# Pool branch of a decoder layer: band matrices on TensorE against running sums on VectorE

## The chip, the cores and the metric

One core of a Trainium2 chip runs one launch of the kernel. The metric is device microseconds of one execution; the times given are medians of several.

## The reference

A trunk of two layers (DEPTH = 2) over 256 tokens and a width of 2048, all in float32. The part of a layer that matters here is the mixer: one input projection gives 1024 pool columns, 512 columns for q, 512 for kv and 64 for the key rope. The pool columns go through four causal means, one per group of 256 columns:

```
def multiscale_pool(u, pool_w, pool_scale):
    cs = jnp.cumsum(uf, axis=1)
    for g, w in enumerate((2, 4, 8, 16)):
        c = cs[..., g * POOL_C:(g + 1) * POOL_C]
        lag = jnp.pad(c, ((0, 0), (w, 0), (0, 0)))[:, :S]
        cnt = jnp.minimum(t + 1, w)
        outs.append((c - lag) / cnt)
    diff = pooled - u                      # per group
    y = einsum('bsgc,gcd->bsgd', diff, pool_w) * pool_scale

u = rms_norm(h, norm_mix_g[i]) @ w_in[i]
y_pool = multiscale_pool(u[..., :1024], ...)
y_att = latent_attention(u[..., 1024:1536], u[..., 1536:2048], u[..., 2048:], ...)
h = h + concat([y_pool, y_att]) @ w_out[i]
h = h + conv_gated_ffn(...);  h = h + (p[i] @ w_ple[i]) * sigmoid(...)
```

## The kernel before

Products are made in two parts: every weight and every activation is split into a rounded part (hi, fp32r) and the rest (lo), and three products hi x hi, lo x hi, hi x lo are summed in PSUM (`three`, lines 1607 to 1611).

**Weights.** SP loads chunks of 128x2048 into four slots. Each chunk is two halves of 128x1024. ScalarE rounds a half to `w_hi` (`split`, line 648, copy at L658), VectorE subtracts to `w_lo` (`split`, line 1075, L1085). `steps(l, a, b)` splits halves a + 4 to b + 3 of the layer; six halves are held, and a split waits until TensorE has used the half six before. `halves(l, m)` on TensorE waits for the low part of half m. The order of splits, evictions and everything else is written out by hand for each engine: what stands in between on VectorE or ScalarE delays the next split. Halves of a layer: 0 to 7 q latent, 8 to 19 kv latent and key rope, 20 to 27 and 28 to 35 pool, 36 and 37 q rope, 38 to 41 q, 42 to 45 k, 46 to 49 v, 50 and 51 pool_w, 52 to 83 w_out.

**PSUM.** `acc` is two tiles of two banks, taken in turn by blocks (`free_acc`, `block_split`); `tps` is four banks taken in turn by jobs (`new_job`, `jobs_split`).

**Two ways to run a projection.** By token (`square_half`, line 1627): activations 128x128 are stationary, weights of 512 columns move, 96 products of 512 columns in a block of 512 outputs. By row of weights (`by_rows`, line 1963, the gate and up blocks of the FFN): weights 128x128 are stationary, and both parts of the activations of 256 tokens move in one product of 512 columns (`wide`, L1971), the low weights in one of 256 (`half`, L1981); 64 of each in a block. There the normed scale of a token is a row, made by transposing (`rows_spread`).

**The pool branch.** Both pool blocks run by token. `pooled(i)` evicts a block: ScalarE scales by the token's norm factor and rounds (L800), VectorE subtracts (L1097). `diffs(i)` on TensorE (line 1753) multiplies the block by band matrices, which hold mean minus identity for each window: five products for each of four feature tiles (L1766 to L1770). ScalarE rounds the result (L808) and VectorE subtracts (L1096). The first `diffs` stands after two halves of the second pool block, the second after the q projection. GpSimd builds the bands at the start (lines 522 to 537) and finishes them in `band_parts` (line 550).

**Order on TensorE around it:** key rope block, five halves of pool block 0, transposes of the key rope and of the kv latent (10), three halves, two halves of pool block 1, `diffs(0)`, six halves, q rope (`qrope`), q (`qnope`), `diffs(1)`, k (`knope`), transposes of q rope, v, then scores of head 0, `pool_out`, and the heads. Before the scores TensorE waits for the eviction of the first v block (`block_split(l, BL["v"])`, line 1895).

**Order on VectorE from the q block on:** eviction of q (two blocks, `qk`), splits 44 and 45, `diffs(1)`, splits 46 and 47, eviction of k (two blocks), splits 48 and 49, four subtractions of the q rope, splits 50 and 51, eviction of v (two blocks, two subtractions each), splits 52 and 53, softmax of head 0.

Of the kernel before, what the change touches and what calls it, by code (L numbers as in the profile page):

```python
# [27 lines left out]
P = 128  # L28
F32 = mybir.dt.float32
# [3 lines left out]
ALU = mybir.AluOpType  # L33
# [12 lines left out]
POOL_SETUP = 44 + 4 * len(POOL_WINDOWS) + 4 * len(POOL_WINDOWS)  # L46
# [11 lines left out]
def layer_plan(d_model, d_ff):  # L58
# [26 lines left out]
    for name, n in (("cq", 1), ("pool", 2)):  # L85
        for i in range(n):
            last[block[name] + i] = 2 * (chunk[name] + (i + 1) * per_block) - 1
    last[block["ckv"]] = 2 * chunk["ckr"] + 5
# [33 lines left out]
def build(nc, x, p, positions, norm_mix_g, w_in, pool_w, pool_scale, q_norm_g, w_uq, kv_norm_g, w_ukv,  # L122
# [26 lines left out]
    TURNS = JOBS - (ROWS_JOBS - 1) - FFN_JOBS - (P_JOBS - 1)  # L149

    def turned(l, job):

        n = job
        for name, skipped in (("rows", ROWS_JOBS - 1), ("ffn", FFN_JOBS), ("p", P_JOBS - 1)):
            if job > JB[name]:
                n -= skipped
        return TURNS * l + (n + 1)
# [12 lines left out]
    with ExitStack() as ctx:  # L170
# [11 lines left out]
        band_lo = sb("band_lo", [P, len(POOL_WINDOWS), 16], F32R)  # L182
# [16 lines left out]
        band_hi = sb("band_hi", [P, len(POOL_WINDOWS), 3 * P], F32R)  # L199
# [15 lines left out]
        with ExitStack() as scope:  # L215
# [3 lines left out]
            band = sb("band", [P, len(POOL_WINDOWS), 3 * P], scope=scope)  # L219
            inv_cnt = sb("inv_cnt", [P, 16], scope=scope)  # L220
# [7 lines left out]
        with ExitStack() as scope:  # L228
# [12 lines left out]
            with ExitStack() as early:  # L241
                up_ = (sb("upool_hi", [P, TT, BLK], F32R, scope=early),
                       sb("upool_lo", [P, TT, BLK], F32R, scope=early))
# [56 lines left out]
        upool_hi = sem("upool_hi")  # L300
        diff_hi = sem("diff_hi")
        qr_step = sem("qr_step")
# [38 lines left out]
        STEPS = 4 + 2 + 2 + 4 + 5  # L341

# [155 lines left out]
        def _(pool):  # L498
# [26 lines left out]
            pool.wait_ge(dve_setup, 1)  # L525
            for g, w in enumerate(POOL_WINDOWS):
                step(pool.tensor_copy(band[:, g, 0:w], inv_cnt[:, 0:w]))
            after()
            for g, w in enumerate(POOL_WINDOWS):
                for c0, cn in ((0, 2 * P), (2 * P, P)):  # L530
                    b = band[:, g, c0:c0 + cn]
                    step(pool.affine_select(out=b, in_=b, compare_op=ALU.is_ge, fill=0.0, base=0,
                                            pattern=[[1, cn]], channel_multiplier=-1))
                    after()
                    step(pool.affine_select(out=b, in_=b, compare_op=ALU.is_ge, fill=0.0, base=w - 1,
                                            pattern=[[-1, cn]], channel_multiplier=1))
            after()
# [11 lines left out]

            def band_parts():  # L550
                for g in range(len(POOL_WINDOWS)):
                    for c0 in (0, 2 * P):
                        step(pool.tensor_tensor(band[:, g, c0:c0 + P], band[:, g, c0:c0 + P], ident[:, :],
                                                ALU.subtract))
                after()

                step(pool.tensor_copy(band_hi[:, :, :], band[:, :, :]))
                after()
                step(pool.tensor_tensor(band_lo[:, :, :], band[:, :, 0:16], band_hi[:, :, 0:16].bitcast(F32),
                                        ALU.subtract))  # L560
                assert n[0] == POOL_SETUP
# [24 lines left out]
            for l in range(L):  # L586
# [4 lines left out]
                if l == 0:  # L591
                    band_parts()
# [43 lines left out]
        def _(act):  # L636
# [84 lines left out]
            for l in range(L):  # L721
# [74 lines left out]
                def pooled(i):  # L796
                    b = BL["pool"] + i
                    block_ready(act, l, b)
                    for t in range(TT):
                        copy(up_[0][:, t, :], acc[b % 2][:, t, :], ACT.Copy,  # L800
                             scale=rstd["mix"][:, t:t + 1]).then_inc(upool_hi, 1)

                def diffs(i):
                    for k in range(2):
                        job = JB["diff"] + 2 * i + k
                        act.wait_ge(t_ready, turned(l, job))
                        kt = DIFF + 4 * i + 2 * k
                        copy(xb[0][:, kt:kt + 2, :].rearrange("p a b -> p (a b)"), tps[:, job % T_BANKS, :],  # L808
                             ACT.Copy).then_inc(diff_hi, 1)

                pooled(0)
                steps(l, 28, 30)
                diffs(0)
                steps(l, 30, 36)
# [14 lines left out]
                steps(l, 40, 42)  # L829
                diffs(1)  # L830
                steps(l, 42, 44)
# [3 lines left out]
                for i in range(2):  # L835
# [4 lines left out]
                    copy(q_both[ROPE:P, 2 * i:2 * i + 2, 1, :], pair[ROPE:P], ACT.Copy).then_inc(qr_hi, 1)  # L840
                steps(l, 46, 48)
# [206 lines left out]
        def _(dve):  # L1048
# [17 lines left out]

            step(dve.memset(k_lo[ROPE:P, 0, :].bitcast(F32), 0.0))
# [87 lines left out]
            for l in range(L):  # L1155
# [48 lines left out]
                dve.wait_ge(kr_step, 3 * l + 2)  # L1204
                dve.tensor_copy(kr_tok[:, :, ROPE:P], kr_tok[:, :, 0:ROPE]).then_inc(kr_step, 1)
# [4 lines left out]
                bank = tps[:, JB["kr"] % T_BANKS, 0:S]  # L1210
                lo(k_lo[0:ROPE, 0, :], bank[0:ROPE], k_hi[0:ROPE, :])
# [4 lines left out]

                def pooled(i):
                    b = BL["pool"] + i
                    for t in range(TT):
                        dve.wait_ge(upool_hi, 2 * TT * l + TT * i + t + 1)  # L1220
                        lo(up_[1][:, t, :], acc[b % 2][:, t, :], up_[0][:, t, :],
                           rstd["mix"][:, t:t + 1]).then_inc(acc_free[b % 2], 1)

                def diffs(i):
                    for k in range(2):
                        job = JB["diff"] + 2 * i + k
                        dve.wait_ge(diff_hi, 4 * l + 2 * i + k + 1)
                        kt = DIFF + 4 * i + 2 * k
                        two = lambda x: x[:, kt:kt + 2, :].rearrange("p a b -> p (a b)")
                        lo(two(xb[1]), tps[:, job % T_BANKS, :], two(xb[0])).then_inc(t_done, 1)  # L1230
# [3 lines left out]
                diffs(0)  # L1234
                steps(l, 30, 36)
# [36 lines left out]
                diffs(1)  # L1272
# [3 lines left out]
                steps(l, 44, 46)  # L1276
# [8 lines left out]
                steps(l, 46, 48)  # L1285
# [311 lines left out]
        def _(pe):  # L1597
# [91 lines left out]
            for l in range(L):  # L1689
# [54 lines left out]
                square_halves(l, m, b, xa, 0, 5)  # L1744
                pe.wait_ge(kr_step, 3 * l + 3)
                bank = new_job(l, JB["kr"])
                for t in range(TT):
                    ins = pe.transpose(bank[:, t * P:(t + 1) * P], kr_tok[:, t, :], ident[:, :])
# [4 lines left out]
                def diffs(i):  # L1753

                    if i == 0:
                        pe.wait_ge(pool_setup, POOL_SETUP)
# [393 lines left out]
```

## Time and profile before

| what | value |
|---|---|
| median of 3 runs | 2195.02 us (2194.47 to 2195.32) |
| the profiled execution's own time | 2194.54 us |
| its span, first to last instruction | 2192.8 us |
| TensorE busy | 2180.4 us, 11639 products |
| VectorE busy | 1475.3 us |
| ScalarE busy | 1045.6 us |
| GpSimd busy | 61.7 us |
| granted TensorE clock, mean | 0.999 |

The times in the rows count from the start of the span. In a timeline a row is a run of like instructions: start, length, engine, line, operation, tiles, shape, count, and in brackets the idle time before it with what ended it. Products overlap: one of 512 columns is shown with 0.39 us, but the next starts about 0.227 us after it, so the cost of a run is read from the starts.

### The profile page before, as it was taken

How to read it: one execution, taken by the hardware profiler on the slowest of the kernel's cores; microseconds unless marked ns; L12 is line 12 of the kernel's file. 1: busy time of each engine (PE TensorE's matmuls, PEld its weight loads, DVE VectorE, ACT ScalarE, POOL GpSimd, SP SyncE). 2: the span in 40 equal slices, each digit the busy share in tenths (PEclk: the TensorE clock that was granted, in tenths of full speed). 3: DMA queues.
4: the chain of work that ended last, by engine and by line, in shares of the span. 5: the costliest groups of instructions: out<-in, count | busy, mean ns of one | idle time of the engine just before them, and what ended most of it. 6: DMA issues, size and time to landing. Idle time of an engine off the chain costs nothing.

```text
span 2192.8 us, 32099 instructions
## 1 busy us (share of the span) xinstructions
PE 2180.4 (99%) x11639; PEld 1888.9 (86%) x11639; DVE 1475.3 (67%) x1852; ACT 1045.6 (48%) x1338; POOL 61.7 (3%) x144
## 2 busy tenths in 40 slices
PE   9999999999999999999999999999999999999998
PEld 8898888888888888888898988888888888888886
DVE  6577567766677766676556765677666677766764
ACT  6555444444444443445554554444443444444554
POOL 5000000000000000000000000000000000000011
PEclk9999999999999999999999999999999999999999
DMA  7644555555555555555556355555555555555562
GB/s 258 204 148 154 192 191 182 195 185 191 191 192 191 191 191 188 195 172 193 189 171 187 131 177 184 186 194 189 191 191 191 191 191 191 188 183 189 181 217 96
DMA packets 232987, 406.44 MB, mean 185 GB/s; under 512 B 14780, under 2 KB 49708, under 8 KB 232792
## 3 DMA queue, kind: packets, MB, share of 16 engines
q1 hardware_dynamic: 231824, 402.68, 55.4%
q0 software_dynamic: 512, 1.76, 0.3%
q10 hardware_dynamic: 584, 1.11, 0.1%
q8 instruction: 42, 0.69, 0.1%
q14 instruction: 25, 0.20, 0.0%
HBM read 403.42 MB, written 2.10 MB: 185 GB/s over the span
## 4 chain that ended last, share of the span: by engine, by line
PE 99%; issue 0%; DVE 0%; ACT 0%; POOL 0%; POOLq 0%; ACTq 0%
PE acc L1971 15%; PE tps L1971 15%; PE acc L1609 14%; PE acc L1611 14%; PE acc L1610 14%; PE tps L1981 8%; PE acc L1981 8%; PE tps L1610 4%; PE tps L1611 4%; PE tps L1609 4%; PE tps L1666 1%; PE tps L1602 0%; PE tps L1875 0%; DVE w_lo L1085 0%; PE tps L1855 0%
## 5 line engine op out<-in xcount | busy, mean ns | idle before, releaser
L1085 DVE TENSOR_TENSOR w_lo<-raw,w_hi 128x1024 fp32r<-128x1024 f32 (+1 forms) x768 | 920.3, 1218 | 450.9 <-ACT w_hi L913 309.2
L913 ACT ACTIVATE w_hi<-raw 128x1024 fp32r<-128x1024 f32 x508 | 529.4, 1059 | 664.4 <-PE acc L1971 129.7
L1971 PE MATMUL acc<-xa,w_hi 128*128 128x512 f32 x1408 | 333.5, 390 | 0.0
L658 ACT ACTIVATE w_hi<-raw 128x1024 fp32r<-128x1024 f32 (+1 forms) x260 | 262.1, 1042 | 147.9 <-PE acc L1611 143.0
L1971 PE MATMUL tps<-xa,w_hi 128*128 128x512 f32 x1408 | 331.1, 390 | 0.0
L1971 PEld LDWEIGHTS tps<-xa,w_hi 128*128 128x128 f32 x1408 | 261.5, 188 | 52.4
L1971 PEld LDWEIGHTS acc<-xa,w_hi 128*128 128x128 f32 x1408 | 260.8, 188 | 52.3 <-DVE h L1350 0.4
L1609 PE MATMUL acc<-w_hi,xb_hi 128*128 128x512 f32 x560 | 220.7, 394 | 0.0
L1611 PE MATMUL acc<-w_lo,xb_hi 128*128 128x512 f32 x560 | 218.2, 390 | 0.0
L1610 PE MATMUL acc<-w_hi,xb_lo 128*128 128x512 f32 x560 | 217.8, 389 | 0.0
L1981 PEld LDWEIGHTS acc<-xa,w_lo 128*128 128x128 f32 x1408 | 175.5, 191 | 3.9
L1981 PEld LDWEIGHTS tps<-xa,w_lo 128*128 128x128 f32 x1408 | 174.7, 192 | 3.4
L1981 PE MATMUL acc<-xa,w_lo 128*128 128x256 f32 x1408 | 176.7, 283 | 0.0
L1981 PE MATMUL tps<-xa,w_lo 128*128 128x256 f32 x1408 | 175.8, 283 | 0.0
L1609 PE MATMUL acc<-w_hi,xa 128*128 128x512 f32 (+1 forms) x384 | 139.5, 363 | 1.5 <-DVE xa L1097 1.5
L1611 PE MATMUL acc<-w_lo,xa 128*128 128x512 f32 (+1 forms) x384 | 137.7, 359 | 0.0
L1610 PE MATMUL acc<-w_hi,xa 128*128 128x512 f32 (+1 forms) x384 | 137.4, 358 | 0.0
L1609 PE MATMUL acc<-w_hi,gt_hi 128*128 128x512 f32 x320 | 124.5, 389 | 0.0
L1610 PE MATMUL acc<-w_hi,gt_lo 128*128 128x512 f32 x320 | 124.5, 389 | 0.0
L1611 PE MATMUL acc<-w_lo,gt_hi 128*128 128x512 f32 x320 | 124.5, 389 | 0.0
L1609 PE MATMUL tps<-w_hi,gt_hi 128*128 128x512 f32 x320 | 124.5, 389 | 0.0
L1610 PE MATMUL tps<-w_hi,gt_lo 128*128 128x512 f32 x320 | 124.5, 389 | 0.0
(224 smaller groups left out, 2499.9 us busy)
## 6 DMA issues: line engine op xcount, KB each, us to landing
raw<-in_w_up SPq DMA_DIRECT2D x176, 1024.0 KB, 4.9
raw<-in_w_down SPq DMA_DIRECT2D x88, 1024.0 KB, 4.9
raw<-in_w_out SPq DMA_DIRECT2D x32, 1024.0 KB, 5.0
raw<-in_w_ple_gate SPq DMA_DIRECT2D x32, 1024.0 KB, 4.9
raw<-in_w_in SPq DMA_DIRECT2D x22, 1024.0 KB, 5.3
raw<-in_w_ukv SPq DMA_DIRECT2D x8, 1024.0 KB, 5.4
raw<-in_w_in SPq DMA_DIRECT2D x8, 864.0 KB, 4.8
raw<-in_w_uq SPq DMA_DIRECT2D x6, 1024.0 KB, 5.6
```

What stands on the lines that cost most here:

```text
L658: copy(w_hi[:, half_of(m), 0:n], raw[:, c % RAW_SLOTS, at:at + n], ACT.Copy).then_inc(hi_done, 1)
L913: copy(w_hi[:, half_of(m), :], raw[:, c % RAW_SLOTS, (m % 2) * HALF:(m % 2 + 1) * HALF], ACT.Copy).then_inc(hi_done, 1)
L1085: dve.tensor_tensor(w_lo[:, half_of(m), 0:n], raw[:, c % RAW_SLOTS, at:at + n], w_hi[:, half_of(m), 0:n].bitcast(F32), ALU.subtract).then_ ...
L1609: pe.matmul(dst, a_hi, b_hi, start=first, stop=False)
L1610: pe.matmul(dst, a_lo, b_hi, start=False, stop=False)
L1611: return pe.matmul(dst, a_hi, b_lo, start=False, stop=last)
L1666: ins = pe.transpose(bank[:, i * S + t * P:i * S + (t + 1) * P], tiles(t, i), ident[:, :])
L1971: ins = pe.matmul(dst, hi[:, k * BLK + n * P:k * BLK + (n + 1) * P], x_both[:, kt, :, :].rearrange("p a s -> p (a s)"), start=kt == 0, sto ...
L1981: ins = pe.matmul(bank(n, False)[:, S:2 * S], lo[:, k * BLK + n * P:k * BLK + (n + 1) * P], xa[0][:, kt, :], start=False, stop=False)
```

## The change

TensorE now runs both pool blocks by row of weights: the left one (halves 20 to 27) in the four banks of `acc`, the right one (28 to 35) in the four banks of `tps`. The result has features on partitions and tokens along the row. The norm factors come as a row: VectorE spreads the factor of each token over a 128x128 tile, two more transposes turn them, and `mix_row` keeps them. `pooled(i)` copies the low sums on ScalarE and adds the high sums on VectorE into `u_pool[i]`, with 16 zeroed columns ahead of the tokens. `by_mix_row(i)` multiplies by the factors. `windows(i, k)` doubles a running sum by additions of a shifted copy (one addition for window 2, two for 4, three for 8, four for 16), corrects the first tokens, and takes u from the scaled sum. `diffs(i, k)` rounds on ScalarE and subtracts on VectorE as before, from SBUF. Band matrices, band products and `band_parts` go. Before `pool_out` TensorE waits for all four differences. On VectorE, `windows(1, 1)` stands between the splits of halves 48 and 49, and the subtractions of the right half's differences between 50 and 51.

```
TensorE
-                square_halves(l, m, b, xa, 0, 5)
+                by_rows(m, left_bank, 0, 6, None, 2)
                 pe.wait_ge(kr_step, 3 * l + 3)
...
+                for t in range(TT):
+                    ins = pe.transpose(bank[:, S + t * P:S + (t + 1) * P], u_pool[1][:, t, PAD:PAD + P], ident[:, :])
                 turn_lat(1, JB["ckv"])
-                square_halves(l, m, b, xa, 5, 8)
-                square_halves(l, m, b, xa, 0, 2)
-                diffs(0)
-                square_halves(l, m, b, xa, 2, 8)
+                by_rows(m, left_bank, 6, 8)
+                by_rows(m + 8, right_bank, 0, 8)
...
                 by_feature(m, BL["qnope"], LAT_Q)
-                diffs(1)
                 jobs_split(l, JB["ckv"] + 1)
...
                     if i == 0:
+                        pe.wait_ge(diff_lo, 4 * l + 4)
                         pool_out(0)

by_rows, first two halves of the left block
+                        if cautious == 2 and i == 0:
+                            for j in range(2):
+                                halves(l, m + j, v)
+                            for ns in ((0, 1), (2, 3)):
+                                for j in range(2):
+                                    wide(j, ns)
+                                    ins = half(j, ns)

ScalarE
+                        for k in range(2):
+                            block_ready(act, l, b)
+                            copy(u[:, 2 * k:2 * k + 2, :], acc[b % 2][:, :, S:2 * S], ACT.Copy).then_inc(u_lo, 1)
+                    else:
+                        halves_used(act, l, 2 * CH["pool"] + 15)
+                        copy(u[:, 0:3, :], tps[:, 1:4, S:2 * S], ACT.Copy).then_inc(u_lo, 1)
+                        copy(u[:, 3, :], tps[:, 0, S:2 * S], ACT.Copy).then_inc(u_lo, 1)
...
                 pooled(0)
-                steps(l, 28, 30)
-                diffs(0)
-                steps(l, 30, 36)
+                steps(l, 28, 33)
+                diffs(0, 0)
+                diffs(0, 1)
+                steps(l, 33, 36)
...
-                steps(l, 40, 42)
-                diffs(1)
-                steps(l, 42, 44)
+                steps(l, 40, 44)
...
+                diffs(1, 0)
+                diffs(1, 1)
                 steps(l, 46, 48)

VectorE
+                for t in range(TT):
+                    dve.tensor_scalar(u_pool[1][:, t, PAD:PAD + P], ident[:, :], 0.0, rstd["mix"][:, t:t + 1], ...)
+                dve.tensor_copy(mix_row[:, :], tps[:, JB["kr"] % T_BANKS, S:2 * S]).then_inc(win_step, 1)
...
+                def windows(i, k):
+                    w = POOL_WINDOWS[2 * i + k]
+                    src, shift, flip = u, 1, 0
+                    while shift < w:
+                        win_ready()
+                        win_next(dve.tensor_tensor(to[:, :, PAD:PAD + S], src[:, :, PAD:PAD + S],
+                                                   src[:, :, PAD - shift:PAD + S - shift], ALU.add))
+                        src, shift, flip = to, 2 * shift, 1 - flip
+                    win_ready()
+                    win_next(dve.scalar_tensor_tensor(first, first, float(w), inv_cnt[:, 0:w]..., ALU.mult, ALU.mult))
+                    win_ready()
+                    dve.scalar_tensor_tensor(u[:, :, PAD:PAD + S], src[:, :, PAD:PAD + S], 1.0 / w,
+                                             u[:, :, PAD:PAD + S], ALU.mult, ALU.subtract).then_inc(diff_done, 1)
...
                 pooled(0)
                 steps(l, 28, 30)
-                diffs(0)
-                steps(l, 30, 36)
+                by_mix_row(0)
+                windows(0, 0)
+                steps(l, 30, 31)
+                windows(0, 1)
+                steps(l, 31, 33)
+                diffs(0, 0)
+                diffs(0, 1)
+                steps(l, 33, 36)
                 pooled(1)
                 steps(l, 36, 38)
...
                 steps(l, 40, 42)
-                diffs(1)
+                by_mix_row(1)
+                windows(1, 0)
                 steps(l, 42, 44)
                 qk(BL["knope"], K_T, 4)
                 qk(BL["knope"] + 1, K_T + 4, 6)
-                steps(l, 44, 46)
+                steps(l, 44, 45)
+                windows(1, 1)
+                steps(l, 45, 46)
...
-                steps(l, 46, 48)
+                steps(l, 46, 47)
+                diffs(1, 0)
+                diffs(1, 1)
+                steps(l, 47, 48)

GpSimd
-            for g, w in enumerate(POOL_WINDOWS):
-                step(pool.memset(band[:, g, :], 1.0 / w))
...
+            pool.wait_ge(x_landed[1], 16)
             with nc.allow_non_contiguous_dma(reason="256 positions, once"):
                 pool.dma_start(pos_i[:, :], ...)
...
-                if l == 0:
-                    band_parts()
```

## Rows read from the trace of the kernel before

**Rows 1.** The page: busy time by engine, and the chain that ended last by engine

```profile
PE 2180.4 (99%) x11639; PEld 1888.9 (86%) x11639; DVE 1475.3 (67%) x1852; ACT 1045.6 (48%) x1338; POOL 61.7 (3%) x144
...
PE 99%; issue 0%; DVE 0%; ACT 0%; POOL 0%; POOLq 0%; ACTq 0%
```

**Rows 2.** Stretches: length, busy time of PE, PEld, DVE, ACT, POOL, clock, DMA share, GB/s

```profile
62.68:109.75 47.07, 47.07 (x224) 39.46 (x223) 26.45 (x35) 22.89 (x33) 1.08 (x3) 1.00 0.69 208
...
76.31:77.40 1.09, 1.09 (x11) 1.09 (x10) 0.26 (x1) 0.58 (x2) 0.00 (x0) 1.00 0.05 17
...
91.11:93.34 2.23, 2.23 (x22) 2.22 (x20) 0.31 (x1) 0.60 (x1) 0.00 (x0) 1.00 0.53 143
...
126.71:128.94 2.23, 2.23 (x23) 2.23 (x21) 1.29 (x2) 2.03 (x4) 0.00 (x0) 1.00 0.03 10
...
1149.18:1196.25 47.07, 47.07 (x224) 39.47 (x223) 26.46 (x35) 22.89 (x33) 1.08 (x3) 1.00 0.66 188
```

**Rows 3.** Timeline of TensorE: k products, fourth half of v, first scores

```profile
130.90 0.28 PE L1610 MATMUL acc<-xb_hi,w_lo 128*128 128x256 f32 x1
131.02 0.28 PE L1611 MATMUL acc<-xb_lo,w_hi 128*128 128x256 f32 x1
131.39 0.38 PE L1609 MATMUL acc<-xb_hi,w_hi 128*128 128x256 f32 x1
...
145.87 0.40 PE L1609 MATMUL acc<-w_hi,xb_hi 128*128 128x512 f32 x1
...
152.69 0.22 PE L1609 MATMUL tps<-xa 128*128 128x128 f32 x1
```

**Rows 4.** Timeline of ScalarE after the q products

```profile
126.91 1.09 ACT L824 ACTIVATE xa<-acc 128x512 fp32r<-128x512 f32 x2 [4.67 <-PE acc L1611]
127.88 2.01 ACT L658 ACTIVATE w_hi<-raw 128x1024 fp32r<-128x1024 f32 x2
```

**Rows 5.** Timeline of VectorE from the q products to the eviction of v

```profile
128.97 2.36 DVE L1085 TENSOR_TENSOR w_lo<-raw,w_hi 128x1024 fp32r<-128x1024 f32 x2
...
143.10 2.36 DVE L1085 TENSOR_TENSOR w_lo<-raw,w_hi 128x1024 fp32r<-128x1024 f32 x2
...
150.73 1.29 DVE L1096 TENSOR_TENSOR v_lo<-acc,v_hi 128x512 fp32r<-128x512 f32 x2
```

**Rows 6.** Timeline of TensorE: gate and up blocks of the FFN's first unit

```profile
265.61 1.07 PE L1971 MATMUL acc<-xa,w_hi 128*128 128x512 f32 x4
...
271.46 1.03 PE L1666 MATMUL tps<-ident,h 128*128 128x128 f32 x8
272.25 2.07 PE L1971 MATMUL acc<-xa,w_hi 128*128 128x512 f32 x8
...
289.31 3.79 PE L1971 MATMUL tps<-xa,w_hi 128*128 128x512 f32 x16
...
311.53 0.84 PE L1971 MATMUL acc<-xa,w_hi 128*128 128x512 f32 x3
```

**Rows 7.** VectorE by line and shape, 62 to 153 us: busy us, mean ns

```profile
L1085 DVE TENSOR_TENSOR w_lo<-raw,w_hi 128x1024 fp32r<-128x1024 f32 x29 | 34.6, 1222 | 9.5 <-ACT w_hi L658 8.9
...
L1097 DVE SCALAR_TENSOR_TENSOR upool_lo<-acc,rstds,upool_hi 128x512 fp32r<-128x512 f32 x4 | 2.8, 747 | 7.6 <-ACT upool_hi L800 7.6
...
L1096 DVE TENSOR_TENSOR xb_lo<-tps,xb_hi 128x512 fp32r<-128x512 f32 x4 | 2.7, 686 | 3.0 <-ACT xb_hi L808 3.0
```

**Rows 8.** Timeline of VectorE: key rope, the third row waits for the second

```profile
63.78 0.22 DVE L1199 TENSOR_TENSOR kr_tok<-kr_in,cos 128x64 f32<-128x64 f32 x1
63.91 0.22 DVE L1200 TENSOR_TENSOR kr_tmp<-kr_in,sin 128x64 f32<-128x64 f32 x1
64.16 0.22 DVE L1202 TENSOR_TENSOR kr_tok<-kr_tok,kr_tmp 128x64 f32<-128x64 f32 x1
```

**Rows 9.** Timeline of TensorE: warm-up and first product

```profile
2.12 5.68 PE L1602 MATMUL tps<-ident 128*128 128x128 f32 x32 [2.12 <-POOL ident L514]
...
10.45 0.50 PE L1609 MATMUL acc<-w_hi,xa 128*128 128x512 f32 x1 [1.47 <-DVE xa L1097]
```

More of the change, by code:

```diff
@@ L87, in layer_plan @@
             last[block[name] + i] = 2 * (chunk[name] + (i + 1) * per_block) - 1
+    for i in range(2):
+        last[block["pool"] + i] = 2 * chunk["pool"] + 7
     last[block["ckv"]] = 2 * chunk["ckr"] + 5
@@ L148, in build @@
     FFN_JOBS = JB["p"] - JB["ffn"]
-    TURNS = JOBS - (ROWS_JOBS - 1) - FFN_JOBS - (P_JOBS - 1)
+    POOL_JOBS = 4
+    TURNS = JOBS - POOL_JOBS - (ROWS_JOBS - 1) - FFN_JOBS - (P_JOBS - 1)
     def turned(l, job):
         n = job
-        for name, skipped in (("rows", ROWS_JOBS - 1), ("ffn", FFN_JOBS), ("p", P_JOBS - 1)):
+        for name, skipped in (("diff", POOL_JOBS), ("rows", ROWS_JOBS - 1), ("ffn", FFN_JOBS), ("p", P_JOBS - 1)):
             if job > JB[name]:
@@ L241, in build @@
             with ExitStack() as early:
-                up_ = (sb("upool_hi", [P, TT, BLK], F32R, scope=early),
-                       sb("upool_lo", [P, TT, BLK], F32R, scope=early))
+                u_pool = [sb(f"u_pool{i}", [P, 4, PAD + S], scope=early) for i in range(2)]
             prob = sb("prob", [P, 2, 3 * P], scope=scope)
@@ L341, in build @@
         STEPS = 4 + 2 + 2 + 4 + 5
+        WIN_STEPS = 1 + 2 * (2 + 1) + sum(w.bit_length() for w in POOL_WINDOWS)
         def half_of(m):
@@ L548, in _ @@
                     lat_landed, 16)
[L550 to L561, printed above, removed]
             def factor(done, src, dst, n_terms, step0, halved=False):
@@ L796, in pooled, with diffs @@
                 def pooled(i):
[L797 to L809, printed above, removed]
+                    u = u_pool[i][:, :, PAD:PAD + S]
+                    if i == 0:
+                        for k in range(2):
+                            b = BL["pool"] + k
+                            block_ready(act, l, b)
[4 more added lines that the diff above has]
+                        copy(u[:, 3, :], tps[:, 0, S:2 * S], ACT.Copy).then_inc(u_lo, 1)
+                def diffs(i, k):
+                    act.wait_ge(diff_done, 4 * l + 2 * i + k + 1)
+                    kt = DIFF + 4 * i + 2 * k
+                    copy(xb[0][:, kt:kt + 2, :], u_pool[i][:, 2 * k:2 * k + 2, PAD:PAD + S], ACT.Copy).then_inc(
+                        diff_hi, 1)
                 pooled(0)
-                steps(l, 28, 30)
-                diffs(0)
-                steps(l, 30, 36)
+                steps(l, 28, 33)
+                diffs(0, 0)
+                diffs(0, 1)
+                steps(l, 33, 36)
                 pooled(1)
@@ L1215, in _ @@
                 steps(l, 26, 28)
-                def pooled(i):
[L1218 to L1224, printed above, removed]
-                    for k in range(2):
[L1226 to L1230, printed above, removed]
+                n_win = [WIN_STEPS * l + 1]
@@ L1745, in _, with left_bank, right_bank @@
+                def left_bank(n, first):
+                    if first and n % 2 == 0:
+                        free_acc(l, BL["pool"] + n // 2)
+                    return acc[(BL["pool"] + n // 2) % 2][:, n % 2, :]
+                def right_bank(n, first):
+                    assert JB["diff"] % T_BANKS == 1
+                    return new_job(l, JB["diff"] + n) if first else tps[:, (JB["diff"] + n) % T_BANKS]
+                by_rows(m, left_bank, 0, 6, None, 2)
                 pe.wait_ge(kr_step, 3 * l + 3)
```

196 lines of the change are left out of this document (107 added, 89 removed).

## The prediction

> **What bounds the kernel now.** I read the busy shares first: TensorE is busy 99% of the span, and the chain of waits lies on it for 99% too [rows 1]. So only two things change the time: what TensorE issues, and when it must wait. Every other engine counts only where TensorE waits for it. Next I read the stretches around the change. The pool columns, from the first of their weight halves to the first product with w_uq, take 47.07 us in either layer [rows 2], with TensorE busy throughout, so what holds for one layer is counted twice. In it lie the ten transposes of the key rope and the latent rows (1.09) and the first pair of band products (2.23); the second pair, 2.23 again, stands between the q and k projections [rows 2]. Last I read one engine at a time where TensorE reaches weights that VectorE has barely finished [rows 3 to 5]: there a moved instruction can cost.
>
> A measurement of this kernel can tell some 0.2%, or 4.4 us, from no change.
>
> **Step 1: columns by feature instead of by token.** Each block of 512 pool columns now runs as the gate and up blocks do: 64 products of 512 columns and 64 of 256, in place of 96 of 512. The columns streamed are equal. Before, the 16 halves cost 47.07 - 1.09 - 2.23 = 43.75 us. The up block of the first unit takes 311.53 - 289.31 = 22.22 [rows 6]; that is the right block. The left one has the order of the first gate block, which changes often between the two widths; that took 289.31 - 265.61 = 23.70, of which the eight transposes are 272.25 - 271.46 = 0.79, so 22.9 at most. As that still holds two more transposes and a wait for VectorE, I take 22.4. Sum 44.6, which is 0.87 more per layer (bounds 0.7 to 1.4). Two more transposes for the row of norm factors: 0.1 each, 0.2 in all.
>
> **Step 2: no band products before w_uq.** 2.23 us less per layer [rows 2]. Steps 1 and 2 give -2.23 + 0.87 + 0.2 = -1.15 per layer, -2.3 in all.
>
> **Step 3: no band products between q and k.** Here I take nothing, though 2.23 us of products go. The k projection uses halves 42 to 45 of its weights in its first 2.9 us. Halves 44 and 45 are split late: ScalarE first evicts the last q block (from 126.91), which waits for the end of the q products, and only then rounds 44 and 45 (127.88 to 129.89) [rows 4]; VectorE subtracts them from 128.97 to 131.33 [rows 5]. TensorE reaches half 45 at 131.39, after a gap of 0.37 between starts where 0.12 is usual [rows 3]: it waits for that half already. Without the band products it starts the k projection at 126.71, does halves 42 and 43, and waits for 44 and 45, which hang on the end of q by the same chain. The fourth half starts 4.68 us after the end of q either way. Bounds: 0 to -2.5 per layer (the 2.23 and the wait); I take 0, since both ends of this chain are in the rows.
>
> **Step 4: the window sums on VectorE.** Those of the left half (windows 2 and 4) run beside the right block. VectorE is busy 26.45 of the 47.07 us [rows 2]; the change adds some 6.5 us net, by the durations of [rows 7], and follows each piece by splits that TensorE uses at least 5 us later (half 34, the nearest, is ready about 9 us into the right block and used after 16). I cost this at nothing; if that cover failed, each late us would be a us of TensorE. The evictions of the right block hold up halves 40 and 41, ready about 5 us after the right block and used after 7. Window 8 stands before the eviction of the first k block, which then ends some 2 us later than now, still 2 us before v takes its bank.
>
> Window 16 does not fit. It stands on VectorE between the splits of halves 48 and 49, the last two of the v weights. Now 48 and 49 end at 143.10 + 2.36 = 145.46 [rows 5], and TensorE starts half 49's products at 145.87 [rows 3]: 0.4 us to spare. Inserted are four additions of 128x512, one small product for the first 16 tokens and one scaled subtraction of 128x512. A 128x512 subtraction takes 0.686, a scaled one 0.747 [rows 7]. Each addition waits for the one before. The price of such a wait is in [rows 8]: two independent steps start 0.13 apart (63.78, 63.91), a dependent one 0.25 after the step before it, its 0.22 and 0.03 more. So 4 x (0.69 + 0.03) + 0.25 + 0.67 = 3.80 us; the last is not waited for by split 49. Half 49 is then ready at 149.26, TensorE starts at 149.32 (0.06 after, as it did at 131.39) and waits **3.45 us**. The bounds: steps that overlap as independent ones, 0.6 apart, give 3.15; steps slower by a fifth give 4.5. I take 3.80, since the rows are of the same operation and size.
>
> The Trainium skill ("VectorE: DVE Perf Modes", section "The DRAIN you can't avoid") says that a semaphore after each of a chain of Vector operations costs nothing extra; by it the insertion would be about 3.2 us and the whole change +5.1 us in place of +6.4. The 0.25 against 0.13 of [rows 8] speaks against it here.
>
> What is late next: the v products end at 152.69 + 3.45 = 156.14, and TensorE then waits for the eviction of the first v block before the scores. VectorE ended that at 150.73 + 1.29 = 152.02, which is 6.56 us after split 49, with four subtractions and splits 50 and 51 between. The two subtractions of the right half's differences come in among these, 0.6 us each: 149.26 + 6.56 + 1.2 + 0.06 = 157.08, so TensorE waits **0.9 us** more (bounds 0 to 1.3). Queued behind is softmax of the first head; VectorE comes to it 3.8 + 1.2 later at most and TensorE 4.35 later, with pool products of 5.8 us between, so I count nothing.
>
> Per layer 3.45 + 0.9 = 4.35, twice 8.7.
>
> **Step 5: costed at nothing.** GpSimd builds no bands. Its set-up lay beside TensorE's warm-up, and the first product waited for VectorE's part of xa, not for bands [rows 9]; the cleared pads on VectorE fall into its wait for the first gains. GpSimd's six small transfers now wait for the second piece of x instead of for the bands, the piece that TensorE itself needs for its next transposes, and are used only after the first block. No weight transfer is moved on SP's queue; those behind half 49 start 3.8 us later, with chunks two ahead in hand.
>
> **Sum.** -2.3 + 0 + 8.7 = **+6.4 us**. The profiled execution took 2194.54 (span 2192.8), 0.48 under the median of 2195.02; its sum is 2200.9, and on the median's scale **2201.4**.
>
> **Rivals.**
> *The wait at half 49 costs little (not slower).* Its place is the gap between split 48 and TensorE's start on 49; it decides at an insertion of some 2.8 us: below that the two waits of a layer stay under 3.35 us and the time under +4.4. For it: in every other stretch VectorE stands idle and could absorb this. Against: six operations at [rows 7]'s prices do not fit under 3.1. Fully hidden it gives 2195.0 - 2.3 = 2192.7. Chance 0.18, for an order I misjudged.
> *All band products pay (faster).* If ScalarE rounds 44 and 45 before q ends and window 16 hides, 2 x 2.5 more goes: 2187.7. Against it is the chain of [rows 4, 5]. Chance 0.07.
> *TensorE slows after its waits.* After 1.47 us of idling it ran its next products at their usual pace [rows 9]; a wait of 3.45 us stands nowhere in the trace. The 32 transposes of the warm-up took 5.68 us, where 32 at the 0.1 of [rows 6] take 3.2: 2.5 lost at the lower pace. Twice that on top gives 2206.4. Chance 0.08. The Trainium skill ("TensorE: Matmul & The Clock Gate", section "Why this matters for your kernels") warns that idle gaps between bursts bring the clock back to half rate.
> *The windows 2, 4 or 8 hold up a split as well.* One late half of 1 to 3 us a layer: 2203 to 2207. Chance 0.05.
>
> **Numbers.** The forecast has 0.62. Its own range: low with an insertion of 3.15 or no second wait (+4.6 to +5.1), high with 4.5 (+8): 2199.4 to 2203.5. To leave out no more than 2 in 10 the range must take in the hidden case, 2192.0, and reach some way into the last two, 2205.0. Faster by over 0.2%: the second rival and a little, 0.08. Within 0.2%: the first rival, and the forecast's lowest corner, 0.24. Slower: 0.68.
>
> **What would show it.** Right: pool blocks of 22.2 to 22.5 us with no gap between; TensorE idle some 2 us and again 0.4 inside the first k products; idle of about 3.4 us at the fourth half of v, released by VectorE's split; about 0.9 us before the first scores. Wrong: half 49 split before TensorE gets to it, or k products that start their fourth half less than 4.5 us after q; or idle in the right pool block.

## The result and the profile after

The changed kernel takes **2205.11 us** (median of 5 runs, 2203.89 to 2206.00) against 2194.47 us of the kernel before (5 runs beside them): ratio 1.0048, 95% interval 1.0037 to 1.0058. The forecast was 2201.4 us; the direction was right, the time came out 3.7 us longer, just above the range's upper end. The kernel before ran at 2194.47 this time and not at 2195.02, so the change cost 10.6 us where 6.4 were forecast.

The page of the profiled execution (span 2204.1 us) first: busy time by engine, and the chain that ended last. Against [rows 1] VectorE has 24 us more, and 1% of the chain each now lies on VectorE and on issue.

```profile
PE 2181.5 (99%) x11691; PEld 1892.6 (86%) x11691; DVE 1499.3 (68%) x1903; ACT 1044.7 (47%) x1338; POOL 45.2 (2%) x110
...
PE 98%; issue 1%; DVE 1%; ACT 0%; POOL 0%; POOLq 0%; ACTq 0%; DVEq 0%
```

TensorE's waits of the whole span. The first row is new; the other two stand in the kernel before too.

```profile
PE acc L1655 <- DVE w_lo L1069: 10.4, 5, 3.2
PE tps L1648 <- POOL ident L522: 2.1, 1, 2.1
PE acc L1655 <- DVE xa L1081: 1.5, 1, 1.5
```

Stretches of the changed kernel, columns as in [rows 2]; the column to read is the one behind POOL, the granted clock, where 1.00 is the upper of the two levels (2.4 GHz) and 0.50 the lower (1.2 GHz).

```profile
63.20:109.20 46.00, 46.00 (x271) 40.70 (x269) 31.41 (x48) 22.54 (x33) 1.08 (x3) 1.00 0.70 211
...
127.47:129.69 2.22, 0.28 (x3) 0.08 (x1) 2.08 (x4) 2.22 (x3) 0.00 (x0) 1.00 0.01 4
129.69:133.60 3.91, 3.91 (x19) 3.73 (x20) 3.74 (x5) 1.53 (x2) 0.00 (x0) 0.57 0.38 98
...
146.33:149.93 3.60, 0.40 (x3) 0.01 (x1) 3.43 (x7) 2.44 (x5) 0.00 (x0) 1.00 0.00 0
149.93:154.20 4.27, 4.27 (x12) 3.37 (x13) 4.18 (x6) 2.45 (x4) 0.00 (x0) 0.60 0.69 238
154.20:158.49 4.29, 4.29 (x21) 3.51 (x20) 3.40 (x5) 0.00 (x0) 0.00 (x0) 1.00 0.21 47
1221.00:1223.80 2.80, 2.16 (x11) 1.96 (x12) 2.70 (x4) 2.00 (x3) 0.00 (x0) 0.76 0.03 5
1223.80:1226.50 2.70, 2.70 (x17) 2.70 (x16) 2.56 (x5) 0.00 (x0) 0.00 (x0) 0.61 0.92 309
...
1238.30:1241.90 3.60, 0.40 (x2) 0.00 (x0) 3.43 (x7) 2.44 (x5) 0.00 (x0) 1.00 0.01 2
1241.90:1246.40 4.50, 4.49 (x13) 3.57 (x14) 4.41 (x6) 2.47 (x4) 0.00 (x0) 0.62 0.70 233
```

The pool stage is 1.07 us shorter. Then come, in each layer, two stretches with TensorE nearly idle (2.22 and 3.60 us), and behind each of the four a stretch in which it is busy at a clock of 0.57 to 0.76 (the row at 1221.00 still holds the last 0.48 us of its wait). What a fall costs TensorE is its length times the missing share: 3.91 x 0.43 = 1.68, 4.27 x 0.40 = 1.71, 2.80 x 0.24 + 2.70 x 0.39 = 1.72, 4.50 x 0.38 = 1.71. It is 1.7 us each time.

Both places on TensorE's timeline: the end of q and half 45 in k, then half 49 in v and the first scores. The bracket gives the idle time; behind it the starts, 0.23 apart at 146, lie 0.43 apart from 150.74 on.

```profile
126.15 0.28 PE L1655 MATMUL acc<-xb_hi,w_hi 128*128 128x256 f32 x1
...
130.83 0.58 PE L1655 MATMUL acc<-xb_hi,w_hi 128*128 128x256 f32 x1
...
146.10 0.39 PE L1656 MATMUL acc<-w_hi,xb_lo 128*128 128x512 f32 x1
146.33 0.40 PE L1657 MATMUL acc<-w_lo,xb_hi 128*128 128x512 f32 x1
149.93 0.50 PE L1655 MATMUL acc<-w_hi,xb_hi 128*128 128x512 f32 x1 [3.20 <-DVE w_lo L1069]
...
150.74 0.63 PE L1655 MATMUL acc<-w_hi,xb_hi 128*128 128x512 f32 x1
151.17 0.63 PE L1656 MATMUL acc<-w_hi,xb_lo 128*128 128x512 f32 x1
151.59 0.63 PE L1657 MATMUL acc<-w_lo,xb_hi 128*128 128x512 f32 x1
...
158.49 0.22 PE L1655 MATMUL tps<-xa 128*128 128x128 f32 x1
```

VectorE at that time, answering to the row at 143.10 of [rows 5]: the split of half 48, the window of 16, the split of half 49, and further down the eviction of v's first block.

```profile
143.78 1.23 DVE L1069 TENSOR_TENSOR w_lo<-raw,w_hi 128x1024 fp32r<-128x1024 f32 x1
144.93 0.69 DVE L1247 TENSOR_TENSOR win<-u_pool 128x512 f32<-128x512 f32 x1
145.65 2.14 DVE L1247 TENSOR_TENSOR win<-win 128x512 f32<-128x512 f32 x3
147.82 0.19 DVE L1252 SCALAR_TENSOR_TENSOR win<-win,inv_cnt 128x32 f32<-128x32 f32 x1
148.05 0.69 DVE L1256 SCALAR_TENSOR_TENSOR u_pool<-win,u_pool 128x512 f32<-128x512 f32 x1
148.66 1.22 DVE L1069 TENSOR_TENSOR w_lo<-raw,w_hi 128x1024 fp32r<-128x1024 f32 x1
...
156.34 1.29 DVE L1080 TENSOR_TENSOR v_lo<-acc,v_hi 128x512 fp32r<-128x512 f32 x2
```

The insertion lasts from 144.93 to 148.66, 3.73 us, and the split of half 49 ends at 149.88, 0.05 before TensorE goes on.

To compare executions I counted from each one's first product of 512 columns, because that moves from run to run (last experiment). Each entry is a start on TensorE's timeline less that of this product: the first transpose of q's rope part (the end of the k products), the first v product and the first scores. The kernels' names are those of the experiments below.

| us from the first product to | before | changed | window_early | splits_early | filled | before_splits_early | v_first |
|---|---|---|---|---|---|---|---|
| end of k, layer 0 | 130.38 | 130.55 | 130.42 | 126.72 | 129.39 | 130.06 | 126.73 |
| first v product, layer 0 | 131.17 | 131.34 | 131.21 | 127.51 | 130.18 | 130.85 | 127.52 |
| scores, layer 0 | 142.24 | 147.52 | 143.09 | 140.86 | 145.66 | 141.84 | 138.99 |
| scores, layer 1 | 1228.76 | 1239.53 | 1230.89 | 1227.57 | 1235.61 | 1227.93 | 1222.29 |
| (first product at) | 10.45 | 10.97 | 10.73 | 9.99 | 11.13 | 10.18 | 11.08 |

Both layers lose about the same: 5.28 us up to the first scores of layer 0, 10.77 up to those of layer 1, so 5.49 in layer 1. With the later start (0.52) that is the 11.3 us between the spans.

### The profile page after: what moved, and what is told of

It is laid out like the page before. It is cut to its first block, busy times and chain, and to the rows that moved or that the text cites. A ratio compares the mean times of both kernels' runs of the same rounds, so it can differ in the third digit from the quotient of the medians.

```text
span 2204.1 us, 32232 instructions
## 1 busy us (share of the span) xinstructions
PE 2181.5 (99%) x11691; PEld 1892.6 (86%) x11691; DVE 1499.3 (68%) x1903; ACT 1044.7 (47%) x1338; POOL 45.2 (2%) x110
## 4 chain that ended last, share of the span: by engine, by line
PE 98%; issue 1%; DVE 1%; ACT 0%; POOL 0%; POOLq 0%; ACTq 0%; DVEq 0%
PE acc L1799 16%; PE tps L1799 16%; PE acc L1655 12%; PE acc L1657 12%; PE acc L1656 12%; PE tps L1809 8%; PE acc L1809 8%; PE tps L1657 4%; PE tps L1656 4%; PE tps L1655 4%; PE tps L1712 1%; PE tps L1648 0%; DVE win L1247 0%; PE tps L1971 0%; DVE w_lo L1069 0%
## 5 line engine op out<-in xcount | busy, mean ns | idle before, releaser
L1799 PE MATMUL acc<-xa,w_hi 128*128 128x512 f32 x1536 | 366.0, 391 | 0.0
L1799 PE MATMUL tps<-xa,w_hi 128*128 128x512 f32 x1536 | 361.2, 390 | 0.0
L1799 PEld LDWEIGHTS tps<-xa,w_hi 128*128 128x128 f32 x1536 | 285.3, 188 | 57.2
L1799 PEld LDWEIGHTS acc<-xa,w_hi 128*128 128x128 f32 x1536 | 283.7, 188 | 56.2 <-DVE h L1396 0.4
L1809 PEld LDWEIGHTS acc<-xa,w_lo 128*128 128x128 f32 x1536 | 192.7, 191 | 5.1
L1809 PE MATMUL acc<-xa,w_lo 128*128 128x256 f32 x1536 | 194.2, 283 | 0.0
L1809 PE MATMUL tps<-xa,w_lo 128*128 128x256 f32 x1536 | 191.8, 283 | 0.0
L1655 PEld LDWEIGHTS acc<-w_hi,xb_hi 128*128 128x128 f32 x560 | 105.9, 189 | 28.6 <-DVE w_lo L1069 7.6
L1657 PEld LDWEIGHTS acc<-w_lo,xb_hi 128*128 128x128 f32 x560 | 106.0, 189 | 22.6
L1657 PE MATMUL tps<-w_lo,gt_hi 128*128 128x512 f32 x320 | 124.5, 389 | 0.0
```

Source lines behind the costliest of these rows:

```text
L1655: pe.matmul(dst, a_hi, b_hi, start=first, stop=False)
L1657: return pe.matmul(dst, a_hi, b_lo, start=False, stop=last)
L1799: ins = pe.matmul(dst, hi[:, k * BLK + n * P:k * BLK + (n + 1) * P], x_both[:, kt, :, :].rearrange("p a s -> p (a s)"), start=kt == 0, sto ...
L1809: ins = pe.matmul(bank(n, False)[:, S:2 * S], lo[:, k * BLK + n * P:k * BLK + (n + 1) * P], xa[0][:, kt, :], start=False, stop=False)
```

## Experiments

Theory A: the loss is TensorE's two waits in each layer **and** the fall of the granted clock behind each. Rivals: VectorE bounds the stage, so a wait only changes place (B); the products are slow for another reason than the idling, the new VectorE work or the layout (C).

**Window 16 out of the gap (window_early).** VectorE does it where it stood idle:

```
                 qk(BL["knope"], K_T, 4)
-                qk(BL["knope"] + 1, K_T + 4, 6)
-                steps(l, 44, 45)
                 windows(1, 1)
...
-                steps(l, 45, 46)
+                qk(BL["knope"] + 1, K_T + 4, 6)
+                steps(l, 44, 46)
```

> The changed kernel with one move: VectorE does the window of 16 between the evictions of the two blocks of k, where it stood idle for 3.79 us, and no longer between the splits of halves 48 and 49. Theory A (TensorE's idle stretches and the low granted clock behind each make the loss): the wait at half 49 (3.4 us a layer) and the 1.7 us at a granted clock of 0.60 behind it go, twice; VectorE still has the copies of the pool differences ahead of v's first block, so some 0.6 us a layer of waiting come up before the scores: 2205.1 - 2 x (3.4 + 1.7 - 0.6) = 2196, and the granted clock around v is 1.00; around k it still falls to about 0.57. Rival B (VectorE is the bound of the stage, and the 3.7 us are only pushed to another wait): a wait of 2 us or more turns up at k's second block or before the scores, and the time stays above 2202.

Measured: 2197.43 us, ratio to before 1.0012 (1.0003 to 1.0021). The wait at half 49 and the fall behind it are gone in both layers, and the first scores of layer 0 come 4.43 us sooner than in the changed kernel. Of the loss 7.7 us come back, not 9: the wait before the scores took 1.04 between starts, 0.8 more than usual, where 0.6 was expected. Around k the clock still falls in both layers. B is out for this wait. The stretch around v and the wait before the scores, layer 0:

```profile
142.00:153.00 11.00, 11.00 (x50) 8.77 (x48) 10.56 (x15) 8.72 (x13) 0.00 (x0) 1.00 0.28 95
```

```profile
153.82 0.30 PE L1654 MATMUL tps<-xa 128*128 128x128 f32 x1 [0.66 <-DVE v_lo L1080]
```

**The splits too (splits_early).** As above, and on both engines halves 44 and 45 ahead of q's second block, 48 and 49 ahead of k's second (VectorE shown, ScalarE alike):

```
                 qk(BL["qnope"], Q_T, 0)
+                steps(l, 40, 42)
                 qk(BL["qnope"] + 1, Q_T + 4, 2)
-                steps(l, 40, 42)
...
                 windows(1, 1)
...
+                steps(l, 44, 46)
                 qk(BL["knope"] + 1, K_T + 4, 6)
-                steps(l, 44, 46)
```

> As window_early, and ScalarE and VectorE split halves 44 and 45 ahead of the eviction of q's second block, and 48 and 49 ahead of that of k's second block. Theory A: the waits at halves 44 and 45 (together 2.3 us a layer) and the 1.7 us at the low clock behind them go too, and the 0.6 us before the scores: 2196 - 2 x (2.3 + 1.7 + 0.6) = 2187, no granted clock under 0.95 between 109 and 160 us, below both kernels. Rival B: the splits can't start earlier, since they need halves 38 and 39 (42 and 43) used, which comes only at the end of the group before; then the later evictions cost as much as the earlier splits give, and the time is that of window_early, 2196.

Measured: 2193.03 us, ratio 0.9993 (0.9984 to 1.0002), a miss of 6 us. The k stage did what A said (end of k 3.83 us earlier than in the changed kernel, clock 1.00). The scores then met part of what B names, a late eviction: VectorE's of v's first block, still behind splits and differences. TensorE's timeline, and the stretches behind that wait, layer 0 and layer 1:

```profile
148.73 0.39 PE L1657 MATMUL acc<-w_lo,xb_hi 128*128 128x512 f32 x1
150.85 0.30 PE L1655 MATMUL tps<-xa 128*128 128x128 f32 x1 [1.73 <-DVE v_lo L1081]
```

```profile
150.85:155.00 4.15, 4.15 (x24) 4.15 (x25) 4.04 (x9) 1.28 (x2) 0.00 (x0) 0.65 0.69 246
...
1238.00:1243.00 5.00, 5.00 (x44) 5.00 (x44) 3.87 (x10) 1.98 (x5) 0.00 (x0) 1.00 0.65 222
```

The wait is the same in both layers, the fall comes in one only.

**TensorE kept at work while it waits (filled).** The waits stay; transposes that nobody reads fill them:

```
+                def fill(job, count):
+                    for _ in range(count):
+                        pe.transpose(tps[:, job % T_BANKS, 0:P], ident[:, :], ident[:, :])
...
+                                    if k in fills:
+                                        new_job(l, JB["qrope"])
+                                        fill(JB["qrope"], fills[k])
                                     parts.append(halves(l, m + k))
...
-                by_feature(m, BL["knope"], LAT_KV)
+                by_feature(m, BL["knope"], LAT_KV, {2: 16, 3: 3})
...
+                            if k == 3:
+                                new_job(l, JS[0])
+                                fill(JS[0], 28)
                             parts.append(halves(l, m + k))
```

> The changed kernel with the waits left where they are, and TensorE given transposes of the identity that nobody reads while it waits: 16 ahead of half 44 and 3 ahead of half 45 in k, 28 ahead of half 49 in v. Nothing of the chains of ScalarE and VectorE changes. Theory A (the clock falls because TensorE stood idle): the groups of halves 44, 45 and 49 begin when they did, but the granted clock behind them stays at 1.00: 4 x 1.7 us come back, and of them 2 x 0.9 go into the wait before the scores that was forecast: 2205.1 - 6.8 + 1.8 = 2200. Rival C (the products are slow for another reason, such as VectorE and ScalarE working on the same memory, or operands that came late): the products behind the waits stay at 0.213 and 0.427 us, and the time at 2205.

Measured: 2201.9 us, ratio 1.0032 (1.0020 to 1.0044). The v place again:

```profile
145.32 0.39 PE L1657 MATMUL acc<-w_lo,xb_hi 128*128 128x512 f32 x1
145.55 3.22 PE L1892 MATMUL tps<-ident 128*128 128x128 f32 x28
148.94 0.50 PE L1655 MATMUL acc<-w_hi,xb_hi 128*128 128x512 f32 x1 [0.16 <-DVE w_lo L1069]
149.28 0.39 PE L1656 MATMUL acc<-w_hi,xb_lo 128*128 128x512 f32 x1
149.50 0.40 PE L1657 MATMUL acc<-w_lo,xb_hi 128*128 128x512 f32 x1
149.74 0.39 PE L1655 MATMUL acc<-w_hi,xb_hi 128*128 128x512 f32 x1
...
156.79 0.30 PE L1655 MATMUL tps<-xa 128*128 128x128 f32 x1 [0.76 <-DVE v_lo L1080]
```

```profile
129.46:134.00 4.54, 4.34 (x36) 4.03 (x35) 4.37 (x6) 1.99 (x3) 0.00 (x0) 1.00 0.37 97
...
149.00:153.00 4.00, 4.00 (x18) 3.31 (x19) 3.91 (x6) 2.40 (x4) 0.00 (x0) 1.00 0.68 232
```

Half 49's products still begin 3.62 us after the product before the fill, VectorE and ScalarE have the same work, and the products behind run 0.23 apart at a clock of 1.00. So the idling brings the fall; C is out. The gain, 3.2 us, is less than the 6.8 that four falls cost, and less than the 5 expected, for two reasons that the rows show: part of the fall in k lies ahead of half 45, for which TensorE waits anyhow (end of k 1.16 us earlier, not 1.7), and the wait before the scores, foretold at 0.9, appears (1.14 between starts), because the products no longer run late.

**The kernel before without its second band products (before_no_cover, no_cover_again).**

```
+                            if i == 1:
+                                ins = pe.matmul(d[:, 0:16], up_[0][:, 0, f], band_lo[:, g, :], start=True, stop=True)
+                                continue
```

> The kernel before, with the second set of band products (between q and k) cut to one product of 16 columns for each bank: the differences of the last two windows are not computed. Less work for TensorE by 2.2 us a layer, and nothing else changed. Theory A: halves 44 and 45 arrive when they did, so the group of half 45 still begins 4.68 us after the end of q; TensorE stands idle for some 2 us in between, and the granted clock falls behind that: 1.7 us a layer slower with less work, 2194.5 + 3.4 = 2198. Rival C (the fall has to do with the new VectorE work or the by-feature layout): no fall, 2194.5. Rival D (the products did hold up the path after all): 2194.5 - 4.4 = 2190.

> The kernel of before_no_cover once more, unedited: its only trace had idle stretches of 1.78 us and no fall, at 2194.5, while its ten other runs took 2195.4 to 2196.8. Theory A: those are runs with a fall in one layer (1.2 us behind half 45); a second trace with a time near 2196 shows one granted clock near 0.6 behind half 44 or 45, one near 2194.5 shows none. Rival F (they are slower for another reason): a time near 2196 and a granted clock of 1.00 throughout.

Measured: 2196.24 us (11 runs, 2194.51 to 2196.76), ratio 1.0007 (0.9998 to 1.0016); the second traced execution took 2195.69. In the first trace (2194.51 us) both layers wait 1.78 us between starts without a fall, and the end of k, 130.47 us after the first product, is within 0.1 us that of the kernel before. In the second the wait is the same, and in layer 0, not in layer 1, the clock falls; k ends there at 131.91, 1.44 later:

```profile
129.93 0.39 PE L1609 MATMUL acc<-xb_hi,w_hi 128*128 128x256 f32 x1 [1.50 <-DVE w_lo L1085]
131.07 0.39 PE L1609 MATMUL acc<-xb_hi,w_hi 128*128 128x256 f32 x1 [0.16 <-DVE w_lo L1085]
```

```profile
132.00:134.00 2.00, 2.00 (x12) 2.00 (x11) 2.00 (x3) 0.43 (x1) 0.00 (x0) 0.50 0.79 256
...
1219.00:1221.00 2.00, 1.93 (x16) 1.93 (x17) 2.00 (x4) 1.44 (x2) 0.00 (x0) 1.00 0.37 67
```

Two things follow. Taking 2.2 us of products a layer off TensorE there gains nothing, as the forecast's third step said (D is out). And the fall comes without any of the change's VectorE work. It did not come every time, so A's 2198 was too high.

**The same with a longer wait (before_longer_wait).** On ScalarE, in the kernel without those products:

```
-                steps(l, 40, 42)
                 diffs(1)
-                steps(l, 42, 44)
+                steps(l, 40, 44)
```

> The kernel before with the second set of band products cut as in before_no_cover, and ScalarE's two copies of the last two differences moved ahead of its copies for halves 44 and 45, so that these come 0.95 us later: TensorE's idle stretch ahead of half 44 grows from 1.7 to about 2.6 us. In before_no_cover the profiled execution showed no fall of the granted clock behind 1.78 us and took just the time of the kernel before, while the timed ones lay up to 2.3 us higher. Theory A (the fall comes from the idle stretch, and a longer one makes it likelier): a granted clock near 0.6 behind the wait in both layers, and 2194.6 + 2 x (0.95 + 1.2) = 2199. Rival C (only the by-feature kernel has it): granted clock 1.00, and 2194.6 + 2 x 0.95 = 2196.5.

Measured: 2198.58 us, ratio 1.0020 (1.0011 to 1.0029): near A's 2199, and 2.1 above C's. In the trace the fall is again in one layer, not in both, behind equal waits:

```profile
132.05 0.38 PE L1608 MATMUL acc<-xb_hi,w_hi 128*128 128x256 f32 x1 [2.47 <-DVE w_lo L1084]
...
1219.51 0.49 PE L1608 MATMUL acc<-xb_hi,w_hi 128*128 128x256 f32 x1 [2.48 <-DVE w_lo L1084]
```

```profile
133.00:135.00 2.00, 1.83 (x16) 1.81 (x16) 2.00 (x4) 0.58 (x1) 0.00 (x0) 1.00 0.34 39
...
1221.00:1223.00 2.00, 2.00 (x12) 2.00 (x11) 2.00 (x4) 0.03 (x1) 0.00 (x0) 0.50 0.49 120
```

Counted from the first product, k ends 0.98 us later than in the kernel before in the layer without the fall, which is the longer wait, and another 2.02 later in the layer with it. So the fall itself brought 1.04 here, and A's number was met in part by luck: another 0.8 of the traced execution is its late start (first product at 11.28).

**A version without the waits (v_first).** As splits_early, and on VectorE v's first block ahead of the pool differences:

```
-                steps(l, 46, 47)
-                diffs(1, 0)
-                diffs(1, 1)
-                steps(l, 47, 48)
                 for i in range(2):
...
+                    if i == 0:
+                        steps(l, 46, 47)
+                        diffs(1, 0)
+                        diffs(1, 1)
+                        steps(l, 47, 48)
```

> As splits_early, and VectorE evicts v's first block ahead of the split of half 50, the differences of the last two windows and the split of half 51, instead of behind them. In splits_early that eviction ended at 150.65 us and the scores, for which TensorE was free at 148.96, waited for it 2.12 us in each layer, with the granted clock at 0.65 behind it in layer 0 and at 1.00 in layer 1. Theory A: the eviction can end by 147.1, the wait goes, and with it the slow stretch: 2193.0 - 2 x 2.0 - 1.5 (one layer) to 3.0 (both) = 2187, with no granted clock under 0.95 in either layer between q and the scores. Rival B (VectorE's queue is the bound of the whole stage): pool_out then waits for half 50, the differences or half 51 by about as much, and the time stays at 2192 to 2193.

Measured: **2188.88 us**, ratio 0.9972 (0.9961 to 0.9983): faster than both kernels, by 5.7 and 16 us. The eviction row of v now stands before the differences, and the wait before the scores is gone:

```profile
146.89 1.29 DVE L1081 TENSOR_TENSOR v_lo<-acc,v_hi 128x512 fp32r<-128x512 f32 x2
148.10 1.22 DVE L1070 TENSOR_TENSOR w_lo<-raw,w_hi 128x1024 fp32r<-128x1024 f32 x1
149.23 1.29 DVE L1081 TENSOR_TENSOR xb_lo<-u_pool,xb_hi 128x512 fp32r<-128x512 f32 x2
```

B is out: VectorE had room, its order was the trouble. The expected 2187 is missed by 1.9. Between the two traced executions, each near its median, the first scores of layer 1 come 5.28 us sooner than in splits_early, counted from the first product; with one fall to win back, 2 x 2.0 + 1.5 were expected. Another 1.1 of the miss is the start: the first product came at 11.08 here and at 9.99 there. TensorE also reaches half 49 some 0.3 us too early in each layer (0.54 between starts), but it did so in splits_early too.

**The kernel before with the same order of the splits (before_splits_early).**

> The kernel before, with the same two moves of the splits (44 and 45 ahead of the eviction of q's second block, 48 and 49 ahead of that of k's second) and nothing else; the band products stay. Theory A: the band products covered the wait for 44 and 45 but for about 0.3 us a layer, and TensorE has hardly any wait at v, so the moves are worth under 1 us in all: 2194. The distance from here to v_first is then what the change is worth where nothing waits: the 2.23 us of the second band products and the 1.07 us of the pool stage in each layer, 6.6 us. Rival D (the order alone brings it): this kernel comes down to 2190 or less, and the change is worth little.

The edit is that of splits_early without the window. Measured: 2193.55 us, ratio 0.9995 (0.9986 to 1.0004). The order alone brings 1.1 us, not told from none (this run's D, that the order alone brings it, is out); from here to v_first it is 4.7 us in the medians, where 6.6 were expected. In the table k ends 3.33 us earlier in v_first, which is 2.23 + 1.07 = 3.30 of steps 1 to 3, and 0.5 of that is given back up to the scores, 0.3 of it at half 49. The traced execution of v_first also started 0.9 us later: 6.6 less 0.5 in each layer and less 0.9 is 4.7.

**Two more traces, of unedited kernels (after_again, before_again).**

> The changed kernel once more, unedited, for a second trace of it. Theory A (the fall of the clock belongs to the idle stretches): the granted clock falls again behind half 49 in both layers (idle for 3.4 us), and behind halves 44 and 45 in at least one; the first product starts somewhere from 10.0 to 11.3 us, as in the nine traces so far, whichever kernel it is. Rival E (the falls and the 0.52 us later start of the first trace were an accident of one execution): stretches without a fall behind half 49, and a time under 2202.

> The kernel before once more, unedited. What is asked is the start alone: the first product came at 10.45 us in the first trace and at 9.99 to 11.28 in those of the other kernels. If the start is chance, it lies in that range again, though its warm-up and set-up are the same instructions; if it belongs to the kernel, it comes at 10.45 within 0.05, as the 10.40 of before_no_cover did.

Measured: 2205.78 and 2195.29 us. The changed kernel shows the same four falls (0.57, 0.62, 0.66 and 0.62 behind the waits) and first scores 147.46 us after its first product, 0.06 from the first trace. The unedited kernel before started at 11.21 us this time, later than the changed kernel did. The start is chance.

## Why the forecast fell short

- **Steps 1 and 2** (-1.15 us a layer): right. The pool stage went from 47.07 [rows 2] to 46.00 us, -1.07, with TensorE busy throughout; the left block took 22.45 us, the right one 22.23.
- **Step 3** (nothing for the second band products): right in what it says of the chain, and wrong in its price. Half 45 begins at 130.83, 4.68 us after the end of q at 126.15, as foretold. But where there were products TensorE is now idle, and the clock falls. End of k is 0.17 us later instead of 1.07 earlier: 1.24 us in layer 0 that the forecast did not have (1.42 in layer 1). With the wait filled, 1.16 of the 1.24 came back.
- **Step 4, the insertion** (3.80 us, a wait of 3.45): right, with 3.73 and 3.37 (3.60 less the usual 0.23). By the Trainium skill ("VectorE: DVE Perf Modes", section "The DRAIN you can't avoid"), where a semaphore after each operation of a chain costs nothing extra, the forecast's estimate was 3.2. The trace does not agree: the dependent additions start 0.72 apart, and the split, with nothing to wait for, starts 0.61 after the scaled subtraction; the measurement stands.
- **Step 4, the products after the wait**: this is the step that failed, together with the same term in step 3: the pace of TensorE behind its waits was put at the usual one. Behind half 49 the products ran at 1.2 GHz for a while, 1.74 us in layer 0: from the first v product to the scores it was 16.18 us instead of 11.07, of which 3.37 are the wait.
- **Step 4, the second wait** (0.9 us before the scores): did not appear, because TensorE came late itself. The eviction of v's first block ended at 156.34 + 1.29 = 157.63, the scores began at 158.49. With the waits filled it was there, 1.14 between starts.
- **Step 5** (start at nothing): right; the 0.52 us is chance.

The sum of layer 0: the forecast 3.2, plus 1.24 and 1.74 for the clock, less 0.9 for the second wait, makes 5.28, as measured. The third rival, that TensorE slows after its waits, came true in its mechanism. Its 2206.4 lies near the 2205.11 in part by luck: it had one fall of 2.5 us a layer and the second wait, the trace has two falls of 1.7 and no second wait. It was given 0.08 because TensorE ran at its usual pace behind the 1.47 us of [rows 9]. That row was too short a wait to speak for 3.4 us, and the 2 us in k, which the forecast itself foresaw, were not asked about at all. The Trainium skill ("TensorE: Matmul & The Clock Gate", section "Why this matters for your kernels") warned of it, that idle gaps between bursts bring half rate; the 0.60 and 0.62 behind half 49 agree, and the runs here show falls behind shorter waits as well.

Open: what decides in one execution whether a wait of about 2 us brings the fall. Equal waits in the two layers of one trace went both ways.

## What to carry to other kernels

A wait of TensorE cost its length here and, where the clock fell behind it, up to 1.7 us more: in the changed kernel the waits at half 49 took 6.7 us and the falls about 6. Work that is taken off TensorE ahead of a wait with a fixed end gains nothing and opens an idle stretch; move the wait's chain forward first (here the splits ahead of the evictions), then the saved products pay. On an engine with room to spare the place of an insertion in its queue is what counts: moving the window of 16 alone brought 7.7 us back.

## What the runs showed of the hardware

- The granted clock behind idle stretches of TensorE, counted over all the traces by the time between two starts: behind 3.60 us it fell 4 times of 4, behind 2.75 once of 2, behind 2.22 six times of 6, behind 2.12 once of 2, behind 1.78 once of 4, behind 1.04 to 1.15 never of 4. Behind the 1.73 to 1.80 us ahead of the first product of 512 columns [rows 9] it never fell in 12 traces. Each fall cost TensorE 1.7 us, also where only one layer had it (no_cover_again: 2 x 0.08 + 2 x 0.50 + 2 x 0.28 = 1.72 over three stretches); of that, 1.04 (before_longer_wait) to 1.74 us (half 49) reached the products further on.
- Transposes by the identity that nobody reads held the clock at 1.00 through 3.4 us of waiting (filled).
- The same 32 transposes of the warm-up took from 5.29 to 6.52 us, and so the first product came anywhere between 9.99 and 11.28 us, in both kernels. Two traces of it, splits_early and the kernel before in its second trace:

```profile
2.05 5.29 PE L1648 MATMUL tps<-ident 128*128 128x128 f32 x32 [2.05 <-POOL ident L522]
```

```profile
2.12 6.45 PE L1602 MATMUL tps<-ident 128*128 128x128 f32 x32 [2.12 <-POOL ident L514]
```

A difference of up to 1.3 us between two single traces of this kernel is therefore no finding, until the start is taken out.
